# Two of eleven down tiles of the first block's feed-forwards as seven block products, behind the up tiles

## What is computed

```python
def swiglu_ffn(x, w1, w2):
    a, b = jnp.split(x @ w1, 2, axis=-1)
    return (jax.nn.silu(a) * b) @ w2
...
x = x + FFN_RES_WEIGHT * swiglu_ffn(rms_norm(x, ffn1_norm[l]), ffn1_w1[l], ffn1_w2[l])
```

## Time and profile before

| | |
|---|---|
| median of 3 runs | 2240.15 us |
| profiled execution, its own time | 2240.4 us |
| its span | 2238.7 us |
| busy: PE, DVE, ACT | 2222.5 (99%), 1529.8 (68%), 1210.0 us (54%) |
| granted TensorE clock, mean | 0.999 |
| DMA | 409.38 MB, mean 183 GB/s |

### The profile page before, as it was taken

One profiled execution on the slowest core, in us unless ns is written; L12 is line 12 of the kernel. 1 busy time (PEld: TensorE's weight loads), 2 busy tenths in 40 slices (PEclk: granted clock), 3 DMA queues, 4 the chain that ended last, 5 costly groups with the idle time before them and its releaser, 6 DMA issues.

```text
span 2238.7 us, 30449 instructions
## 1 busy us (share of the span) xinstructions
PE 2222.5 (99%) x12350; PEld 1898.8 (85%) x12350; DVE 1529.8 (68%) x2112; ACT 1210.0 (54%) x1812; POOL 67.6 (3%) x118
## 2 busy tenths in 40 slices
PE   8999999999999999999999999999999999999998
PEld 7888987888888889878888988888888988888887
DVE  6557578665665575786656866786777766786766
ACT  6456455454564564555545655455555555455554
POOL 0000000000000000000000200000000100000000
PEclk9999999999999999999999999999999999999999
DMA  8565544455545655434655544445555544445553
GB/s 286 192 232 184 199 180 151 171 188 188 188 186 190 232 186 204 182 144 169 232 189 190 187 151 165 156 153 181 190 192 178 189 151 165 156 166 181 188 188 113
DMA packets 62803, 409.38 MB, mean 183 GB/s; under 512 B 7976, under 2 KB 9512, under 8 KB 15304
## 3 DMA queue, kind: packets, MB, share of 16 engines
q1 hardware_dynamic: 62664, 407.44, 50.5%
HBM read 405.83 MB, written 2.10 MB: 182 GB/s over the span
## 4 chain that ended last, share of the span: by engine, by line
PE 94%; DVE 3%; ACT 1%; DMA 1%; issue 0%; SPq 0%; POOLq 0%; DVEq 0%; POOL 0%; ACTq 0%
PE bank L593 20%; PE bank L594 20%; PE bank L595 20%; PE bank L640 18%; PE bank L647 9%; DVE w_lo L270 1%; PE bank L393 1%; PE bank L1733 1%; PE bank L1745 1%; DMA w_raw<-in_tiles 0%; PE bank L2345 0%; PE bank L2052 0%; PE bank L2513 0%; PE bank L2062 0%; PE bank L2072 0%; PE bank L2532 0%
## 5 line engine op out<-in xcount | busy, mean ns | idle before, releaser
L270 DVE TENSOR_TENSOR w_lo<-w_raw,w_hi 128x2048 fp32r<-128x2048 f32 x367 | 835.1, 2284 | 69.0 <-ACT w_hi L240 68.6
L240 ACT ACTIVATE w_hi<-w_raw 128x2048 fp32r<-128x2048 f32 x359 | 685.3, 1912 | 107.7 <-DMA w_raw<-in_tiles 107.5
L640 PE MATMUL bank<-hT,w_hi 128*128 128x512 f32 x1920 | 459.5, 390 | 2.4 <-DVE w_lo L270 2.4
L640 PEld LDWEIGHTS bank<-hT,w_hi 128*128 128x128 f32 x1920 | 355.8, 188 | 73.8 <-DVE w_lo L270 2.8
L593 PE MATMUL bank<-w_hi,hT 128*128 128x512 f32 (+2 forms) x832 | 327.9, 394 | 0.3
L595 PE MATMUL bank<-w_hi,hT 128*128 128x512 f32 (+2 forms) x832 | 318.9, 383 | 0.0
L594 PE MATMUL bank<-w_lo,hT 128*128 128x512 f32 (+2 forms) x832 | 318.8, 383 | 0.0
L647 PEld LDWEIGHTS bank<-hT,w_lo 128*128 128x128 f32 x1920 | 247.7, 191 | 10.3
L647 PE MATMUL bank<-hT,w_lo 128*128 128x256 f32 x1920 | 250.9, 283 | 0.0
L593 PEld LDWEIGHTS bank<-w_hi,hT 128*128 128x128 f32 x832 | 156.8, 188 | 37.6 <-issue 7.9
L595 PEld LDWEIGHTS bank<-w_hi,hT 128*128 128x128 f32 x832 | 156.6, 188 | 31.3
(11 more groups left out here) (395 smaller groups left out, 2984.8 us busy)
## 6 DMA issues: line engine op xcount, KB each, us to landing
w_raw<-in_tiles SPq DMA_DIRECT2D x368, 1024.0 KB, 4.8
a_cmp_w<-in_cmp_w SPq DMA_DIRECT2D x2, 2048.0 KB, 7.8
shifted<-in_bias SPq DMA_DIRECT2D x12, 256.0 KB, 7.2
w_raw<-in_tiles SPq DMA_DIRECT2D x8, 256.0 KB, 5.7
a_gm_rows<-in_rows SPq DMA_DIRECT2D x2, 768.0 KB, 7.0
x_res<-in_x SPq DMA_DIRECT2D x2, 512.0 KB, 5.1
a_ret_rows<-in_rows SPq DMA_DIRECT2D x2, 512.0 KB, 8.0
b_rows<-in_rows SPq DMA_DIRECT2D x2, 512.0 KB, 6.2
```

The lines of the kernel that those rows point to most:

```text
L240: act.activation(k.hi[slot][:], k.raw[slot][:], ACT.Copy).then_inc(k.hi_done[slot], 1)
L270: dve.tensor_tensor(k.lo[slot][:], k.raw[slot][:], k.hi[slot][:].bitcast(F32), ALU.subtract).then_inc(k.lo_done[slot], 1)
L640: pe.matmul(bank[:], k.hi[slot][:, w], k.hT[:, c].rearrange("p a s -> p (a s)"), start=c == 0, stop=False)
```

## The change

Of the eleven down tiles, those of pairs 2 and 3 are computed with Strassen's scheme (in its seven-product, fifteen-addition form). A down tile is a product of a 2 x 2 block matrix of activations (token half x slice) with a 2 x 2 block matrix of weights (slice x 512 columns). Seven products take the place of eight.

- **Weights.** DVE makes the four sums of the weight blocks that the scheme needs: a "made" tile, which takes a ring entry of its own without a load (`Ring.make`, three chained subtractions). It is copied by ACT and split by DVE like a loaded one.
- **Activations.** While pairs 3 and 4 go through, DVE makes four 128x128 sums of the blocks of `g` (`add_blocks`), ACT copies them and DVE splits them.
- **Results.** The seven products go to banks 6, 7, 4 and, once the up tiles are done with them, 2, 3, 0 and 1. After the second Strassen tile DVE adds these up and into x (`recombine`, eight operations of 128x512).
- **Order.** Down tiles 2, 6, 3 and 7 are taken out of the run of pairs and stand behind pair 10's up tiles: 2, made, 6, 3, made, 7, then 9 and 10 as before. The ring has 35 entries for a feed-forward and not 33.

```diff
+            if m + 1 < len(self.places) and self.places[m + 1] is None:
+                dve.wait_ge(k.landed[self.slot[m + 1]], 16 * self.nth[m + 1])
...
+    def make(self, dve, m, link):
+        k, slot, made = self.k, self.slot[m], self.slot[m + 1]
...
+        dve.wait_ge(k.landed[slot], 16 * self.nth[m])
+        dve.wait_ge(k.used[made], self.before[m + 1])
+        link(dve.tensor_tensor(t[:, 0:2], w[:, :, 1], w[:, 0], ALU.subtract))
+        link(dve.tensor_tensor(t[:, 2], w[:, 1, 1], t[:, 0], ALU.subtract))
+        dve.tensor_tensor(t[:, 3], w[:, 1, 0], t[:, 2], ALU.subtract).then_inc(k.landed[made], 16)
...
         norm, ring = self.norm, self.k.ring
         self.add(dve, 0)
+        ring.lo_to(dve, self.end + 1)
         norm.vector_xn(dve, 0)
...
+GATED = Plan((2, 3), (6, 7), (2, 6, 3, 7))
+CONVOLVED = Plan((), (), ())
...
+    def strassen(self, pe, i):
+        ring.ready(pe, n)
+        product(self.acc[0][0], a12, n, 2, False, False)
+        product(self.acc[0][1], s4, n, 3, False, False)
+        ring.ready(pe, n + 1)
+        product(self.acc[1][0], a22, n + 1, 3, False, False)
+        if first:
+            pe.wait_ge(self.summed[0], self.parts(FFN_PAIRS - 1, 1))
+        product(k.bank[2], s2, n + 1, 2, first, last)
+        product(k.bank[3], s3, n + 1, 1, first, last)
+        if first:
+            pe.wait_ge(self.summed[1], self.parts(FFN_PAIRS - 1, 1))
+        product(k.bank[0], a11, n, 0, first, last).then_inc(k.used[ring.slot[n]], 1)
+        product(k.bank[1], s1, n + 1, 0, first, last).then_inc(k.used[ring.slot[n + 1]], 1)
...
                 self.split_hi(act, i, j)
+                if j == 0 and i - 1 in self.plan.strassen:
+                    self.sums_hi(act, i - 1)
+                if self.conv is None and j == 0 and i == FFN_PAIRS - 1:
+                    k.ring.hi_to(act, self.up_at(i, 1) + SLOTS - 1)
             if i < FFN_PAIRS - 1:
                 k.ring.hi_to(act, self.up_at(i, 1) + SLOTS)
+        k.ring.hi_to(act, self.down_at(ENDING[1]) + 1)
...
                 self.add_parts(dve, i, j, 0)
+                ahead = self.conv is None and i == FFN_PAIRS - 1 or self.conv is not None and i == 2 and j == 0
                 ring.lo_to(dve, self.up_at(1, 0) + SLOTS if i == 1 else self.up_at(i, j) + SLOTS - 2 + ahead)
+                if self.plan.strassen and (i, j) == (FFN_PAIRS - 2, 1):
+                    ring.make(dve, self.down_at(self.plan.strassen[0]), link)
                 self.convolve(dve, i, j)
                 self.add_parts(dve, i, j, 1)
+                if self.plan.strassen and (i, j) == (FFN_PAIRS - 1, 1):
+                    ring.make(dve, self.down_at(self.plan.strassen[1]), link)
```

More of the change, by code:

```diff
@@ L706, in up @@
         if i == 1 and j == 1:
-            for first_ok in self.first_ok:
-                pe.wait_ge(first_ok, self.which + 1)
+            pe.wait_ge(self.first_ok, NT * (self.which + 1))
         last = i == FFN_PAIRS - 1
@@ L752, in down, with activations, product @@
         return last
+    def activations(self, i, t, j):
+        if i in self.plan.later:
+            return self.z_hi[i][:, 2 * j + t], self.z_lo[i][:, 2 * j + t]
+        ts = slice(t * P, (t + 1) * P)
+        return self.g_hi[i % 2][j][:, ts], self.g_lo[i % 2][j][:, ts]
+    def strassen(self, pe, i):
+        k, ring, n = self.k, self.k.ring, self.down_at(i)
+        a11, a12, a22, s1, s2, s3, s4 = range(7)
+        first, last = i == self.plan.strassen[0], i == self.plan.strassen[-1]
+        def product(bank, block, tile, q, start, stop):
+            w, slot = slice(q * 512, (q + 1) * 512), ring.slot[tile]
+            return three_passes(pe, bank[:], (self.z_hi[i][:, block], self.z_lo[i][:, block]),
+                                (k.hi[slot][:, w], k.lo[slot][:, w]), start, stop)
+        ring.ready(pe, n)
[11 more added lines that the diff above has]
+        product(k.bank[1], s1, n + 1, 0, first, last).then_inc(k.used[ring.slot[n + 1]], 1)
     def tensor(self, pe, following):
@@ L765, in tensor @@
                     self.turn(pe, 1)
[L766 to L771, removed]
-                last.then_inc(used(i - 1), 1)
+            if i - 1 not in self.plan.tail + ENDING:
+                self.whole(pe, i - 1)
+        if self.plan.strassen:
+            pe.wait_ge(self.chain, self.links + 4 * len(self.plan.strassen))
+        for i in self.plan.tail:
+            if i in self.plan.strassen:
+                self.strassen(pe, i)
+            else:
+                self.whole(pe, i)
         if following is None or following.by_columns:
@@ L785, in tensor, with whole @@
                     last.then_inc(used(i), 1)
+    def whole(self, pe, i):
+        k = self.k
+        k.ring.ready(pe, self.down_at(i))
+        for j in range(2):
+            pe.wait_ge(self.glo_done[j], self.base + i + 1)
+            for t in range(NT):
+                last = self.down(pe, i, t, j)
+        last.then_inc(k.used[k.ring.slot[self.down_at(i)]], 1)
     def end_by_columns(self, pe, following):
@@ L865, in split_hi @@
         act.wait_ge(self.g_done[j], self.base + i + 1)
+        if i in self.plan.tail:
+            out, g = self.parts_of(self.z_hi, i, j)
+            act.activation(out, g, ACT.Copy).then_inc(self.ghi_done[j], 1)
+            return
         if i >= 2:
-            self.k.ring.wait_used(act, self.down_at(i - 2), 1)
+            before = max(h for h in range(i) if h % 2 == i % 2 and h not in self.plan.tail)
+            self.k.ring.wait_used(act, self.down_at(before), 1)
         act.activation(self.g_hi[i % 2][j][:], self.g[j][:], ACT.Copy).then_inc(self.ghi_done[j], 1)
```

140 lines of the change are left out of this document (113 added, 27 removed).

## The result

| | before | after |
|---|---|---|
| median | 2240.26 us (4 runs) | 2252.27 us (2251.82 to 2252.59, 4 runs) |
| ratio | | 1.0054, 95% interval 1.0041 to 1.0066 |
| span of the profiled execution | 2238.7 us | 2250.1 us |
| busy: DVE, POOL | 1529.8, 67.6 us | 1599.8, 73.5 us |

The changed kernel is slower by 12.0 us (0.5%), where +6.0 was forecast. The sign was right; the time lies above the range. The profiled execution of the changed kernel is the fastest of its four, so its span has grown by 11.4 us and not by 12.0.

The account below looks back on a forecast made before the run. PE's own work was taken as the bound: -5.5 us for 24 matmuls, 2 x 1.6 and 2 x 3.8 for tails, +0.7 for joins, sum +6.0 on 2240.15, giving 2246.2 us; range 2241.0 to 2249.5.

Parts of the forecast that it names:

- The small loads: First feed-forward of each layer: mixer loads delay the first make's tile; PE ends that late tail 3.8 us late.
- The make: DVE's three chained subtractions for a made tile: 2.60 us, floor 2.20, ceiling 2.87.
- the second make: Tail, before pair 10's last g: runs t = 14.53 to 17.13, delaying g, ACT's copies and splits of 30 and 31.
- Rival (b): Small loads don't hold the make; all four tails cost 1.6 us, 2241.8 us in all; chance 0.15.
- Rival (a): Makes hide in DVE's idle time, PE never waits and the gain arrives: 2235.4 us; chance 0.13.
- the split of 31: DVE's split of the second Strassen tile's made partner: wanted at t = 22.77, forecast done at 24.35 in plain tails.
- the tails: Ends of four feed-forwards: PE late 1.6 us in two plain ones, 3.8 us in two late ones.
- the 10 to 11 announced: Sign: PE waits before product a11's bank and entries 30 and 31, 10 to 11 us over four feed-forwards.
- I am wrong if PE's waits for w_lo stay under some 5 us: The prediction's own sign of failure: PE's total waits for w_lo under some 5 us.
- the price of the joins: Three joins, ring split now between residual add and xn: 0.25 us each, +0.7 us in all.
- the join between the blocks: Join between the two blocks: said to keep its order, so no cost was added.
- Rival (c): Late recombination or landings push the join 1 or 2 us each, or PE's clock drops (2.0 us): about 2250; chance 0.10.

Follow-up runs that it names:

- e6: New tile order alone, down tiles 2, 6, 3, 7 plain, without makes, block sums or recombination; ring split ahead of the residual add: 2240.54 us, 1.0003.
- e1: Changed kernel with the second make's three subtractions moved from ahead of pair 10's last g to behind it: 2248.22 us.
- e2: Changed kernel with the mixer's small loads issued behind the first Strassen tile's load, not ahead of it: 2246.92 us.
- e3: Changed kernel with the ring split between residual add and xn moved ahead of the residual add at three joins: 2247.40 us.
- e4: Kernel before the change, with the ring split behind xn moved between the residual add and xn at eight joins: 2248.99 us, 1.0039.
- e5: Changed kernel with second make behind g, small loads behind the first Strassen tile's load, and ring split ahead of the residual add, together: 2242.50 us.
- e7: Changed kernel with second make behind g, small loads later, split ahead of the residual add, and one Strassen tile per feed-forward: 2244.26 us.

## Why the prediction was wrong

**Right.** PE is the bound, and only its matmuls and its waits count: -5.5 us. The small loads hold the first make, which moves the whole tail: 8.0 us for 7.6. The make takes 2.65 us (600.53 to 603.18) where 2.60 was taken; by the page of the Trainium skill that the prediction names it would be 2.36. The block sums cost PE nothing. The order costs nothing that can be told (e6). Taken away one by one, the second make and the small loads gave back about what they were said to cost (e1, e2). Rival (b) falls: DVE's first make waits for a DMA in the first feed-forward of each layer and in no other, as forecast. Rival (a) falls as well. Its point, the split of 31 ready by t = 22.8, is missed by 1.7 us, by the chain that was named; e1 shows that two exchanged steps are enough to reach it. PE's printed waits in the tails are 6.6 us and not the 10 to 11 announced, since the lateness of 11.7 us lies partly in slow matmuls and in the longer distance behind each wait, and since a wait is printed from the end of the matmul before it, 0.16 us later than the next one would have started. By its own sign ("I am wrong if PE's waits for w_lo stay under some 5 us") the prediction was wrong here too: those waits are 3.2 us in the tails, and the sign did not allow for this. The size of the tails, read from the starts, was right within 0.9 us. With the make at its ceiling the stated terms add up to 2248.0 and not 2248.1.

**The step that failed** is the price of the joins: "which frees DVE for the split at about 191.8; with 2.20 more xn starts at 194.0 and not 193.66", 0.25 us each. It followed DVE's queue and took the time of `x_rstd` as given. But the moved split stands exactly where GpSimd makes `x_rstd`, and holds it. Each join cost 1.5 us, three of them 4.5 for 0.7 (e3, e4). These 3.8 us are the largest part of the 5.4 by which the span missed the sum; the tails are 0.9 of it, the join between the blocks 0.9, the rest -0.2. The kernel before had shown it, in rows that were not read. POOL's timeline of the kernel before, at the join between the blocks:

```profile
1240.00 2.15 POOL L581 TENSOR_SCALAR x_double<-x_double 128x1 f32<-128x1 f32 x1
```

and DVE's, where a split is under way:

```profile
1239.79 2.28 DVE L270 TENSOR_TENSOR w_lo<-w_raw,w_hi 128x2048 fp32r<-128x2048 f32 x1
```

An operation on 128x1 that elsewhere takes 0.22 us takes 2.15 us, until the split is done.

**The second miss**, 0.9 us, is "the join between the blocks keeps its order". It does, but not its start. DVE's timeline of the changed kernel:

```profile
1244.04 1.23 DVE L262 TENSOR_TENSOR w_lo<-w_raw,w_hi 128x1024 fp32r<-128x1024 f32 x1
1245.18 0.68 DVE L1102 SCALAR_TENSOR_TENSOR x_res<-bank,x_res 128x512 f32<-128x512 f32 x1
...
1249.68 0.69 DVE L566 TENSOR_TENSOR a_xn<-x_res,a_grow 128x512 f32<-128x512 f32 x1
```

and POOL's:

```profile
1249.83 0.98 POOL L604 TENSOR_TENSOR x_double<-x_double,neg_half 128x1 f32<-128x1 f32 x1
```

The recombination and the half split behind it leave DVE to the first add at 1245.18, without a wait and 0.6 us later against PE than before; and an operation of GpSimd that now falls under a DVE operation with two SBUF operands (1249.68) takes 0.98 us, where it took 0.57. Rival (c) had named a late recombination, at a price of 1 or 2 us. e2 shows that it depends on the landings: there the same join is not late. At the three other joins that part of rival (c) is not what happened, although its time of about 2250 is near: the residual add still waited for PE (1.43 us before the row at 193.75), so the recombination was not late there.

**The clock.** Rival (c) gave 2.0 us to a fall of the clock in the waits of the late tails. In the first feed-forward it fell. PE's timeline of the changed kernel:

```profile
169.22 0.50 PE L610 MATMUL bank<-w_hi,f_ffn_z_hi 128*128 128x512 f32 x1 [1.81 <-DVE a_ffn_b L1060]
...
170.73 0.62 PE L610 MATMUL bank<-w_hi,f_ffn_z_hi 128*128 128x512 f32 x1
...
174.14 0.40 PE L612 MATMUL bank<-w_hi,f_ffn_z_lo 128*128 128x512 f32 x1
```

From 170.73 to 174.14 eight matmuls start 0.43 apart, the 1.2 GHz level. In e3 PE had the same wait at the same place, and the clock stayed at 2.4 GHz; but PE then waited for entries 30 and 31:

```profile
169.19 0.50 PE L610 MATMUL bank<-w_hi,f_ffn_z_hi 128*128 128x512 f32 x1 [1.81 <-DVE a_ffn_b L1060]
...
176.84 0.50 PE L610 MATMUL bank<-w_hi,f_ffn_z_hi 128*128 128x512 f32 x1 [0.53 <-DVE w_lo L274]
```

Here are the same six microseconds of both kernels (window, length, PE's busy time, granted clock, DMA share, GB/s), the changed one first:

```profile
169.00:175.00 6.00, 5.78 (x18) 0.72 0.62 217
```

and e3's:

```profile
169.00:175.00 6.00, 5.81 (x25) 1.00 0.61 232
```

The tail is 3.74 us late with the slow matmuls and 3.76 without them. In this tail the fall cost nothing: it filled time in which PE would have waited for DVE. To add it to the waits would have been wrong here.

It moved something else, though. SP may load tile 10 once PE is done with the tile five ring entries ahead of it, tile 6, which was 1.65 us later with the slow matmuls. SP's queue in the changed kernel, then in e3:

```profile
177.99 0.33 SPq L206 DMA_DIRECT2D w_raw<-in_tiles  x1
```

```profile
176.34 0.33 SPq L206 DMA_DIRECT2D w_raw<-in_tiles  x1
```

ACT started on the tile at 182.78 and 181.04, 4.8 and 4.7 us after the issue, so the load itself was not slower. This is why the recombination ended at 192.3 and not at 190.9. In the changed kernel that was still in time; with e3's order the split would then have pushed the residual add. And in e5 a fall at the join between the blocks, with no wait of PE close behind it that it could fill, cost 1.1 us. The Trainium skill ("TensorE: Matmul & The Clock Gate", Part 1) says of a kernel's start that the number of matmuls at the low clock varies from run to run of the same kernel. These two traces, of kernels that are the same up to here, agree: at the start of the program the changed kernel has eight matmuls 0.41 to 0.43 us apart and e3 three. That it varies inside a program too is what the rows above show.

## What to carry to other kernels

When an operation is moved on one engine, look at what every other engine does in that window, and not only at that engine's queue; a small operation of another engine can be the one that is held. Its sign in a profile is a duration that jumps: 2.03 us where the same operation takes 0.22 elsewhere. Costs add up term by term only until the next bound is reached: here the three repairs were worth 9.8 us together, and 14.3 if what each gave alone is added up. A constant that counts queue entries ("eight ahead") has to move with the length of the queue.

## What was not expected of the hardware

- A DVE operation whose operands are both in SBUF holds GpSimd's 128x1 operations for its whole length (2.03 us for 0.22 under a 2.28 us split; 0.45 for 0.19 under a 0.69 us one); one that reads PSUM and SBUF does not (0.22 us under it). That reading from PSUM makes the difference rests on the pairs shown and counted here; it was not tried by itself.
- The first matmul after a wait takes 0.34 us to the next one, not 0.23, in every tail.
- A wait of PE of 1.8 us at the same place was followed by the low clock in one trace and not in three others (e1, e3, e7). A wait of 2.5 us at the join between the blocks was not followed by it (e1), one of 3.0 us was (e5). Why is open; no run was made for it.
- Eight slow matmuls cost nothing where PE would have waited later anyway (the first tail of the changed kernel); slow transposes and the three matmuls behind them cost 1.1 us where it would not (e5).
